# New interleavings of the lanes' steps on TensorE, ScalarE and VectorE in the four mixers of a two-model kernel

## What is computed

```python
for l in range(2):                                   # first model
    mod = (silu(c) @ w_ada[l] + b_ada[l])            # 6144 values: shift, scale, gate, twice
    shift_m, scale_m, gate_m, shift_f, scale_f, gate_f = split(mod, 6)
    h = rms_norm(x, norm_mix[l]) * (1 + scale_m) + shift_m
    x = x + gate_m * hybrid_mixer(h, ...)            # 8 stick-breaking heads, 4 GLA heads, w_out
    h = rms_norm(x, norm_ffn[l]) * (1 + scale_f) + shift_f
    x = x + gate_f * hierarchical_moe(h, ...)        # 4 groups x 8 experts, top 1, then top 2
for l in range(2):                                   # second model
    proj = rms_norm_2(x, norm1_g[l]) @ w_in[l]
    mix = concat(mla, diff, swa, na)                 # four kinds of attention, 4 heads each
    x = x + mix @ w_out[l]
    x = x + square(relu(rms_norm_2(x, norm2_g[l]) @ w_up[l])) @ w_down[l]
return rms_norm_2(x, final_norm_g)
```

## Time and profile before

| | |
|---|---|
| median of 3 runs | 1479.4 us (1476.24 to 1483.46) |
| profiled execution | 1481.0 us, span from first to last instruction 1478.8 us |
| granted TensorE clock, mean | 0.962 |
| TensorE matmuls | 1314.6 us busy, 89% of the span |
| VectorE | 730.4 us, 49% |
| ScalarE | 526.9 us, 36% |
| GpSimd | 50.7 us, 3% |
| HBM | 389.45 MB read, 264 GB/s over the span |

### The profile page before, as it was taken

How to read it: one execution, slowest core, us unless ns; L and a number is a source line. 1 busy time by engine, 2 the same in 40 slices (tenths; PEclk the granted TensorE clock), 3 DMA queues, 4 the chain that set the end, 5 groups by cost and what they waited for, 6 DMA issues and landing times. The chain is left out here.

```text
span 1478.8 us, 21544 instructions
## 1 busy us (share of the span) xinstructions
PE 1314.6 (89%) x9066; PEld 981.4 (66%) x9066; DVE 730.4 (49%) x1126; ACT 526.9 (36%) x894; POOL 50.7 (3%) x46
## 2 busy tenths in 40 slices
PE   5999998766579999976666999999999999999997
PEld 2765674433247667633432778789898878799986
DVE  1744653121146467321111777765555777764554
ACT  3535331000044354200000546654444546644343
POOL 0200000000002000000000110000000110000000
PEclk9999999888899999998887999999999999999999
DMA  9798799999977957999999714456555305455551
GB/s 353 284 334 308 280 413 421 421 421 420 399 283 275 341 200 301 421 421 421 421 393 402 179 32 172 142 156 202 186 193 173 107 3 198 143 168 189 186 198 43
DMA packets 135976, 392.10 MB, mean 265 GB/s; under 512 B 26816, under 2 KB 40128, under 8 KB 111296
## 3 DMA queue, kind: packets, MB, share of 16 engines
q1 hardware_dynamic: 132128, 389.48, 70.7%
q10 hardware_dynamic: 3744, 1.15, 0.4%
HBM read 389.45 MB, written 1.05 MB: 264 GB/s over the span
## 5 line engine op out<-in xcount | busy, mean ns | idle before, releaser
L413 DVE TENSOR_TENSOR spl<-ring,spl 128x2048 fp32r<-128x2048 f32 x65 | 149.3, 2297 | 135.7 <-ACT spl L404 135.7
L536 PEld LDWEIGHTS ps<-hh,spl 128*128 128x128 f32 x1728 | 204.1, 189 | 6.9 <-issue 5.8
L536 PE MATMUL ps<-hh,spl 128*128 128x256 f32 x1728 | 206.2, 280 | 2.8 <-DVE hh L499 2.8
L404 ACT ACTIVATE spl<-ring 128x2048 fp32r<-128x2048 f32 x66 | 126.7, 1920 | 148.3 <-PE ps L536 107.7
L2335 PE MATMUL ps<-spl,ur 128*128 128x512 f32 x768 | 176.7, 389 | 0.0
L2335 PEld LDWEIGHTS ps<-spl,ur 128*128 128x128 f32 x768 | 143.2, 188 | 29.2
L925 DVE TENSOR_TENSOR spl<-ring,spl 128x1024 fp32r<-128x1024 f32 (+2 forms) x120 | 138.4, 1175 | 24.6 <-ACT spl L916 24.2
L1337 PE MATMUL ps<-ring,ar 128*32 128x256 f32 x928 | 98.5, 443 | 57.4 <-issue 25.0
L1337 PE MATMUL ps<-spl_as_slots,ar 128*32 128x256 f32 x864 | 103.8, 479 | 45.1 <-DMA spl_as_slots<-in_w_up 29.3
L916 ACT ACTIVATE spl<-ring 128x1024 fp32r<-128x1024 f32 (+2 forms) x120 | 116.8, 1011 | 49.4 <-DMA ring<-in_w_out 11.7
L516 PE MATMUL ps<-spl,hh 128*128 128x512 f32 x480 | 117.6, 398 | 3.8 <-DVE spl L925 1.3
(11 more groups left out here) (370 smaller groups left out, 1758.5 us busy)
## 6 DMA issues: line engine op xcount, KB each, us to landing
ring<-in_w_up SPq DMA_DIRECT2D x52, 1024.0 KB, 5.3
spl_as_slots<-in_w_down SPq DMA_DIRECT2D x50, 1024.0 KB, 15.4
ring<-in_w_ada SPq DMA_DIRECT2D x48, 1024.0 KB, 7.2
spl_as_slots<-in_w_up SPq DMA_DIRECT2D x40, 1024.0 KB, 17.4
ring<-in_w_gate SPq DMA_DIRECT2D x38, 1024.0 KB, 16.8
ring<-in_w_down SPq DMA_DIRECT2D x38, 1024.0 KB, 4.9
ring<-in_w_in SPq DMA_DIRECT2D x34, 1024.0 KB, 7.5
ring<-in_w_out SPq DMA_DIRECT2D x16, 1024.0 KB, 6.9
```

What stands on the lines that cost most here:

```text
L404: sc.activation(t.hi, t.raw, ACT.Copy).then_inc(s_hi, 2)
L413: v.tensor_tensor(t.lo, t.raw, t.hi, ALU.subtract).then_inc(s_lo, 1)
L536: ins = pe.matmul(ps[:, banks[m // 2], (m % 2) * 256:(m % 2) * 256 + 256], le, ri, start=(kk == 0 and q == 0 and m % 2 == 0), stop=(kk == ...
```

## The change

All twelve strings of `ORDER` but the empty ones of GpSimd are replaced; nothing else in the file changes. In the first model the new strings have no digit 2, the empty lane's, and are shorter for that; the number of steps of each lane is the same.

```diff
--- before.py
+++ after.py
@@ -23,10 +23,10 @@
 PAD = 128
 OUT2 = (1, 0, 2, 3)
 IN1 = (0, 1, 3, 2, 4, 5)
-ORDER = {("mix1", 0, "PE"): "004004000665505005566501525301535005650051255345025314542012513215205054351045551040454250152550054420030040005", ("mix1", 0, "ACT"): "00000406600040566451023500061563500524310021253112321526000135051520602404055043410002640", ("mix1", 0, "DVE"): "000060060406066640656665102630004650031042051231241620045004446534105024064400450412005403",
-         ("mix1", 1, "PE"): "04040000055665000506650215055035053014552531205520045103451415623241005342140255410125000445300020040", ("mix1", 1, "ACT"): "0004000406600540660050061523005600312542531123601000213125320100231056142400445600204", ("mix1", 1, "DVE"): "0004006046006066606566600600512304000652143164502341040021452040360414630412400440502405",
-         ("mix2", 0, "PE"): "4000040040001230010210310243101241234023120413242132401423421031203101213230131420023130132124030023240034201", ("mix2", 0, "ACT"): "00405005000500120031032414102413521523424142031200300101230230141504233201014153402300200344024", ("mix2", 0, "DVE"): "050044000050540123012310550121034024121313242253142414235401400341202312153021153300542132014503102332424311000032220144003", ("mix2", 0, "POOL"): "",
-         ("mix2", 1, "PE"): "4000040004001230010212143010214031232401203341242132401241423031230101312320132140013203230142130332102424000", ("mix2", 1, "ACT"): "00405000050500123124014001032452133214524142010230300012133214510043020312403140035220300441042", ("mix2", 1, "DVE"): "004504005050400123125513101240012004235131234223154241424130401023420312135123155310240032143010321234042135003201020043402", ("mix2", 1, "POOL"): ""}
+ORDER = {("mix1", 0, "PE"): "00400400550506655050505660355540515053505401543505515305531003550414555415410055140150004400000", ("mix1", 0, "ACT"): "0000004604060506650040506543150500036135531013056005315115001060410404400", ("mix1", 0, "DVE"): "00000604040600656666506066006453100504603431050610044415156400034404140045040",
+         ("mix1", 1, "PE"): "0400400055050665500065605531504504501035513045531500015503154014504534104510004040000", ("mix1", 1, "ACT"): "004000046600005665400005613004500631530113005065113010031065410040440", ("mix1", 1, "DVE"): "000000466000046566660606056064100450360311460000535144041064003445144004040",
+         ("mix2", 0, "PE"): "4000000404001320010103214230012141340212320431242132401242143031230101231230310142031230132124030320223400014", ("mix2", 0, "ACT"): "00405005005001002134020314012541323124524104232100300012013231540135400230102143421030220044430", ("mix2", 0, "DVE"): "400050504045001032015532100101234402121313242251354241432140404312020312510350311301253402122431030153241242000303320402410", ("mix2", 0, "POOL"): "",
+         ("mix2", 1, "PE"): "4000040004001203012012124010343120134200231431242132410421423031230101231031232104201303231042311032024043002", ("mix2", 1, "ACT"): "00405000505001020301204140231425133124245140210230300013123210514002034231410354320002001434024", ("mix2", 1, "DVE"): "004500050404512013250512010314220040131351234223142414235401240321403013123512155032012453100431003231243421001023020404230", ("mix2", 1, "POOL"): ""}
 
 
 def layout(parts):
```

## The result

The changed kernel takes 1487.3 us (median of 8 runs, 1484.21 to 1489.44) against 1480.13 us (8 runs, 1476.24 to 1483.46): the ratio is 1.0046, 95% interval 1.0032 to 1.0059. It is slower by 6.8 us by the ratio (7.2 between the medians), where 4.8 less was forecast, and lies outside the range of 1465 to 1484. The profiled execution took 1489.44 us, the longest of the eight, with a span of 1487.2.

A forecast was written before the change was run, and what follows sets the result against it. TensorE was taken to bound the mixers and MLPs, DMA the MoE stretches. First model's mixers -4.1 and 0, second model's -0.7, sum -4.8: 1476.2 against the profiled 1481.0, 1474.6 us against the 1479.4 median; range 1465 to 1484.

The forecast's parts named there:

- What bounds the kernel: TensorE bounds mixers and MLPs, DMA the MoE stretches; a first mixer's saving counts only if the MoE's tile stream starts earlier.
- Mixer 0, -4.1: First model's mixer 0: 9.9 us recoverable less 4.8 of new waits, the rest cut by 1.0; range 0 to -9.9.
- the stretch counted as recoverable: Mixer 0: usual step lengths add to 144.9 of 154.8 us, so at most 9.9 could go, some hidden in stretched groups.
- Mixer 0's waits: New waits in mixer 0: h6.cum 1.0, gla.s1 2.4, ada11.1 0.6, oT0 and out1a 0.8, together 4.8 us.
- The low half of out3 at 180: End of mixer 0: low half of out3 at about 180 instead of 183.8, the MoE's stream starting as much earlier.
- Mixer 1, h6.cum at 0.6 (0 to 2.4): First model's mixer 1: stall of 0.6 us at h6.cum for the moved columns, within 3.8 of new waits against 4.2 recoverable.
- h23.sc, h7.cum and the gate sum, 3.2 together: First model's mixer 1: new waits of 1.7 at h23.sc, 1.0 at h7.cum and 0.5 us at the gate sum.
- The second mixers, -0.7: Second model's mixers, both layers: old waits gone -1.0, new ones at ms.kn +0.3 and +0.5, elsewhere +0.3 each; +4 to -6.
- The fixed cost of 2 us: Skill's estimate for small transfers: columns would land 4.9 us after first issue, 5 us less, some 1469.6; rows spoke against it.
- The slower one, 1489: Rival: VectorE stands at the moved columns, four stalls 12.7 us plus late loads 6; +9, 1489 us; chance 0.14.
- All waits go: Rival: columns land near the least 3.5 us and nothing stands in the mixers; -13, 1466.5 us; chance 0.27.

The follow-up runs named there:

- The digit moved in the experiment: Changed kernel with VectorE's ada16 step in the first model's mixer 1 moved behind h6.sp and two low halves: mixer 138.4 us, kernel ratio to before 0.9996.

## Why the prediction was wrong

- **What bounds the kernel: right, but for a share.** The mixers are TensorE's, and the MoE follows the issue of `w_up`. That "the MoE after it has its full length" holds to 1.1 us in layer 0 and 0.3 in layer 1.
- **Mixer 0, -4.1: the step that failed is the stretch counted as recoverable.** The sum takes TensorE's usual lengths, 144.9 us, as what is left if nothing waits, and so puts 9.9 down as recoverable: 4.85 of idle time and 5.05 of busy time that it calls stretched. Against that it sets 4.8 of new waits and 1.0, so that all the gain forecast is stretch. The runs show no such gain: TensorE's busy time went from 149.95 to 149.27, and over all seventeen traces, old, new and mended, it lies between 148.5 and 151.7. With 149 in place of 144.9 the same waits give 154. Why the usual lengths add up to too little stays open.
- **Mixer 0's waits: their total was right, by luck.** 4.8 were forecast and the six idle times are 4.9. Of the terms, gla.s1 cost 1.2 and not 2.4, h6.cum and the tail no wait of their own on TensorE. In their place came 2.4 for ada tiles in four waits, where I had 0.6 for one of them, from VectorE's stand, and took the others as there in time though TensorE asks for them up to 12 us earlier out of an unchanged list; and 1.35 for ScalarE's copy behind `ada06`, which I hadn't listed among those who wait for VectorE there. The gate sum's wait went, as said.
- **The low half of out3 at 180: wrong, 184.8.** I priced the tail as a stall of TensorE (0.8), and there was none. The cost is in who stands behind whom on ScalarE: out3's high half behind a copy that waits for TensorE's transposes. It took 1.6 us of the stream's lead over the mixer's end (9.14 to 7.55), and the shorter mixer that was to bring the stream 3.8 forward wasn't there. By the means the stream is 1.25 later.
- **Mixer 1, h6.cum at 0.6 (0 to 2.4): the term that cost most.** The landing was right, 8.5 us after the first issue where I took 9.1. The work behind it was not: I counted 1.4 us of VectorE, but a low half stands ahead of the head's step, and it is 2.5 from 502.12 to 504.6. The stall is 2.87, over my upper bound of 2.4, and the lowered clock behind it, which no term of mine had, brought another 1.7. The digit moved in the experiment gives both back. h23.sc, h7.cum and the gate sum, 3.2 together in my sum, cost nothing visible: all but 0.03 of the 2.90 idle in this mixer is the one stall.
- **The second mixers, -0.7: the step that failed is where GpSimd meets VectorE.** I had the collision, and the rule with it, but used it for ms.kn alone. I didn't look which VectorE steps the new places of B30.qk, B21.qk and ms.qperm put under GpSimd's 2.37 us: the first unit's L2170 in mixer 0, with the other unit's steps behind it, an idle time of 2.35 in place of 0.59, and +2.5 for the mixer. Against the old order's other traces, where its one wait is 2.01, the pair is only 0.3 more; there the new order's loss is about 1 us of idle time in all and the clock. ms.kn cost 1.9 in mixer 1 and not 0.5: L2169 and L2170 took 1.86 and 1.19 beside GpSimd, both ahead of L2213. Yet that mixer is 0.8 faster where the clock stays up.
- **The clock.** I read its dips of before and took them as part of the stretched groups. The 1.1 of stretch behind the gate sum's wait, which I counted as recoverable with it, lies in such a dip (busy table of the kernel before):

```profile
166.50:171.50 5.00, 5.00 (x23) 2.17 (x24) 4.36 (x5) 4.20 (x5) 0.00 (x0) 0.66 0.47 160
```

  It went with that wait, as the clock is full over the new mixer 0. But no term had the dips that come behind new stalls: 1.7 in mixer 1, and in the trace of the second mixer 1 another 3.4.
- **The fixed cost of 2 us.** The Trainium skill, "DMA: Bandwidth & Descriptors", section "Anatomy of one DMA", fits this figure to DMAs that GpSimd issues, and these are ScalarE's. In the changed kernel they landed 2.0/6.0/7.5 us after their issue (least, median, most), so "no landing under 3.5" doesn't hold there, and the median does.
- **The rivals.** The slower one, 1489, comes near the measured time, in part by luck. It had one place right, VectorE at the moved columns, but took 12.7 us for its four stalls, and they cost 5.4 (1.35, 1.18, 2.87, and nothing at the fourth) and 1.7 of clock. It took 6 for late loads, where 2.4 came, from the earlier ada steps, and it had the same 144.9 too low a base, and 0.8 for the second mixers, which lost 2.5 in the one and between 1.7 and -0.8 in the other. I gave it 0.14. Its sum also has a slip, 9.0 over 1479.4 being 1488.4. "All waits go" says -13 where its own terms give 14.1 and more; it was no idle thought for mixer 1, which with one digit moved is at 138.4, where the sum without waits was 137.0.

## What to carry to other kernels

When an order of steps is rewritten, the sum of the steps along the new order is a bound, not a forecast: ask at each place where an engine comes to a slow wait (small DMAs, a VectorE step beside a GpSimd instruction) what is queued behind it, and count that work as well. Don't take the sum of usual step lengths for a floor before some trace has come near it. Give a new stall of TensorE two prices, with and without the lowered clock that can follow it (1.7 us or 3.4 here, behind stalls of 1.2 to 2.9, and nothing behind others as long), and don't trust a mended stall until the clock's row has been read too. Strings of several engines are one set: half a set cost 11 us in the one mixer tried, while moving a single step with an eye on one wait gave 5 us.

## What was not expected of the hardware

- The same wait of 1.86 us cost 2.5 us more in one run than in another (142.1 and 139.6), with the granted clock at 0.51 behind it or at 1.00. The old strings of that mixer took 145.1 instead of 140.4 in one trace, at a mean clock of 0.96 and with the same idle times as in the kernel before, the longest of them 0.86, at the mixer's start. So whether a quiet stretch is followed by the lower clock depends on more than its length, and single traces of a stage can differ by as much as a change of order makes.
- L2170 with two operands in SBUF took 0.48 us alone, 2.49 beside GpSimd's L2303, and 1.10 to 1.19 beside its L2308.
- The four small DMAs of a group are slow beside the tiles' stream. From the first issue to the last landing the three groups that VectorE stood for took 8.8, 6.9 and 8.5 us, and all six 5.4 to 10.1 in the kernel before and 3.9 to 9.3 in the changed one. In one view, `--source` of L959 in the changed kernel:

```profile
DMA to landing us min/median/max: 2.0/6.0/7.5
```
